# Whole units in place of half units between the steps of three recurrent mixer chains

## The reference

```python
mod = silu(c) @ ada_w + ada_b                       # six modulation rows of 1024 for each of 9 sequences
h = rms(x) * norm1_w * (1 + sc1) + sh1
proj = h @ w_in                                     # q/k/v/gates of four mixers, then merge gates
A: gated DeltaNet   # causal conv, l2 norm, per tile a triangular solve, 4 heads of 64
B: HGRN2            # per-channel decay, 4 heads of 64
C: Mamba-2 SSD      # causal conv, 8 heads of 32
D: mLSTM            # stabilised, 4 heads of 64
merged = sum_n sigmoid(gate_n) * (rms(mixer_n) * act(z_n)) @ w_branch[n]
x = x + gt1 * (merged @ w_out)
x = x + gt2 * swiglu(rms(x) * norm2_w * (1 + sc2) + sh2)
y = rms(x) * final_norm_w
```

## Time and profile before

| | |
|---|---|
| median of three runs | 1401.7 us (1396.46 to 1403.82) |
| the profiled execution | 1398.09 us, span 1396.3 us |
| PE busy | 1290.7 us, 92% |
| DVE busy | 633.8 us, 45% |
| ACT busy | 381.6 us, 27% |
| mean granted TensorE clock | 0.951 |
| HBM, mean over the span | 83 GB/s |

### The profile page before, as it was taken

The page is one execution under the profiler, slowest core; times in us unless marked ns, Lnnn a source line. Parts: engine busy times, 40 slices in busy tenths (PEclk is TensorE's granted clock), DMA queues, the critical chain, the costliest instruction groups (busy, mean ns, idle before and its releaser), DMA issues. The chain is left out here.

```text
span 1396.3 us, 23271 instructions
## 1 busy us (share of the span) xinstructions
PE 1290.7 (92%) x9849; PEld 1150.7 (82%) x9849; DVE 633.8 (45%) x1240; ACT 381.6 (27%) x561; POOL 12.0 (1%) x30
## 2 busy tenths in 40 slices
PE   5599989999988988999899999996999999989997
PEld 3478768678776766669899999895999999989996
DVE  1341753478788866444433333546222222263332
ACT  1421361552212211034521212114223222251112
POOL 0000100000000000000000000000000000000000
PEclk9799999999999977689999999997999999999999
DMA  9603622222120203025933222231322333223301
GB/s 315 213 16 89 112 92 91 92 91 76 42 66 3 91 1 91 2 67 92 207 85 76 76 76 76 76 85 37 90 81 77 83 90 90 62 83 84 84 22 65
DMA packets 191020, 116.79 MB, mean 84 GB/s; under 512 B 36650, under 2 KB 189351, under 8 KB 190678
## 3 DMA queue, kind: packets, MB, share of 16 engines
q1 hardware_dynamic: 190358, 115.42, 30.0%
q0 software_dynamic: 576, 0.14, 0.1%
HBM read 108.57 MB, written 6.96 MB: 83 GB/s over the span
## 5 line engine op out<-in xcount | busy, mean ns | idle before, releaser
L707 PE MATMUL ps<-scr_parts 128*128 128x272 f32 x2688 | 521.5, 293 | 16.1 <-DVE hT_parts L2213 8.2
L707 PEld LDWEIGHTS ps<-scr_parts 128*128 128x128 f32 x2688 | 429.5, 191 | 20.1 <-issue 13.3
L707 PE MATMUL ps<-hT_parts,scr_parts 128*128 128x272 f32 x1408 | 391.3, 291 | 0.0
L2115 DVE TENSOR_TENSOR scr_parts<-ring,scr_parts 128x1024 fp32r<-128x1024 f32 (+1 forms) x100 | 128.9, 1289 | 305.5 <-ACT scr_parts L1432 302.7
L707 PEld LDWEIGHTS ps<-hT_parts,scr_parts 128*128 128x128 f32 x1408 | 261.8, 190 | 0.0
L707 PE MATMUL ps<-hT,ring 128*128 128x272 f32 x960 | 247.3, 412 | 1.4 <-ACT pj L1306 1.4
L1432 ACT ACTIVATE scr_parts<-ring 128x1024 fp32r<-128x1024 f32 (+1 forms) x100 | 111.0, 1111 | 489.1 <-PE ps L707 488.4
L707 PEld LDWEIGHTS ps<-hT,ring 128*128 128x128 f32 x960 | 185.8, 199 | 43.4 <-issue 4.1
L707 PE MATMUL ps<-pj_parts,scr_parts 128*128 128x272 f32 x992 | 168.1, 294 | 5.7 <-DVEq L1559 5.7
L707 PE MATMUL ps<-scr 128*128 128x128 f32 (+11 forms) x1288 | 138.2, 300 | 14.5 <-DVEq L1559 7.9
L707 PEld LDWEIGHTS ps<-pj_parts,scr_parts 128*128 128x128 f32 x992 | 142.1, 191 | 7.2 <-DVEq L1559 6.3
(11 more groups left out here) (301 smaller groups left out, 1105.8 us busy)
## 6 DMA issues: line engine op xcount, KB each, us to landing
ring<-in_w_in_dram SPq DMA_DIRECT2D x62, 512.0 KB, 6.8
ring<-in_ada_w_dram SPq DMA_DIRECT2D x48, 512.0 KB, 6.5
ring<-in_ffn_w_in_dram SPq DMA_DIRECT2D x44, 512.0 KB, 5.0
ring<-in_ffn_w_out_dram SPq DMA_DIRECT2D x16, 384.0 KB, 3.6
ring<-in_ffn_w_out_dram SPq DMA_DIRECT2D x16, 320.0 KB, 4.1
ring<-in_w_out_dram SPq DMA_DIRECT2D x8, 512.0 KB, 5.0
x_scratch<-scr SPq DMA_DIRECT2D x1, 2176.0 KB, 13.6
Q<-x_scratch SPq DMA_DIRECT2D x1, 2176.0 KB, 10.8
```

Source lines behind the costliest of these rows:

```text
L707: return pe.matmul(out, lhsT, rhs, start=start, stop=stop, skip_group_check=True)
L2115: dve.tensor_tensor(lo, src, hi.bitcast(F32), SUB).then_inc(w_split, 1)
```

## The change

Units are issued whole. The planner gives PE one `product` per unit, with a planned length of 3.7 us for `mix`, 2.1 us for `ada` and 0.9 us for `turn`, and `unit_product(u)` issues all its instructions in a row. The instructions and their waits are the same ones; their order among the steps of the chains is another.

```diff
-                best = (start, "x", unit, f"part{part_}", "pe")
+                best = (start, "x", unit, "product", "pe")
...
-            free[eng] = start + {"mix": 1.85, "ada": 0.9, "turn": 0.9}[SEQUENCE[t][0]]
-            if part_ == 1:
-                evac.append((free[eng], unit))
-                unit, part_ = unit + 1, 0
-            else:
-                part_ = 1
+            free[eng] = start + {"mix": 3.7, "ada": 2.1, "turn": 0.9}[SEQUENCE[t][0]]
+            evac.append((free[eng], unit))
+            unit += 1
...
-            def unit_part(u, part_):
-
-                if part_ == 0 and u >= 2:
+            def unit_product(u):
+
+                if u >= 2:
 
                     pe.wait_ge(x_read, u - 1)
                 kind, v = SEQUENCE[u]
                 if kind == "mix":
                     n, c, h = load_of[("mixer", v // 4)], v // 2 % 2, v % 2
-                    if part_ == 0:
-                        landed(pe, n % R, n)
-                    for k in range(4 * part_, 4 * part_ + 4):
+                    landed(pe, n % R, n)
+                    for k in range(KD):
...
                 elif kind == "ada":
-                    n = load_of[("ada2", 2 * v + part_)]
-                    landed(pe, n % R, n)
-                    last = ada_rows_of(ps[:, u % 2, part_ * 256:(part_ + 1) * 256], n % R)
-                elif part_ == 1:
+                    for e in range(2):
+                        n = load_of[("ada2", 2 * v + e)]
+                        landed(pe, n % R, n)
+                        last = ada_rows_of(ps[:, u % 2, e * 256:(e + 1) * 256], n % R)
+                else:
 
                     pe.wait_ge(x_read, POS[("ada", v)] + 1)
                     for c in range(4):
                         last = mm(ps[:, u % 2, c * 9:(c + 1) * 9], rstd[:, c * P:(c + 1) * P], sum_groups)
-                if part_ == 1:
-                    last.then_inc(x_done, 1)
+                last.then_inc(x_done, 1)
...
-                    unit_part(t, int(name[-1]))
+                    unit_product(t)
```

More of the change, by code:

```diff
@@ L229, in shared_order @@
     ready = {c: 0.0 for c in chains}
-    out, unit, part_, evac = [], 0, 0, []
+    out, unit, evac = [], 0, []
     left = {c: sum(cost(name, eng) + 0.1 for _, name, eng in stages) for c, stages in chains.items()}
```

## The result

The changed kernel takes 1404.0 us (median of 12 runs, 1402.31 to 1408.76), the kernel before 1398.6 us (12 runs, 1396.4 to 1404.38): a ratio of 1.0036, with a 95% interval of 1.002 to 1.0052. It is slower by 5 us. The profiled execution took 1404.93 us with a span of 1403.1 us, 6.8 us over that of before.

The account below looks back on a forecast made before the run. The mixer stage was taken as an account of PE: unit and chain work, idle time and lower clock. Terms 38.2 - 18.6 - 19 - 5 - 3 - 2 + 7 gave -2.4 us, so 1399.3 us against the median; 8-in-10 range 1383 to 1421 us.

Parts of the forecast that it names:

- The point where the units end: Mixer stage: at 1.35 times the units per tile, the 76th unit comes 0.7 through tile 3, about 495 us.
- the units run out early: Rival, chance 0.25: at factor 1.5 the last unit is issued at 443 us of the old trace; +15 us, 1417 us.
- 38.2: Term: unit work from 500 to 605 us and the last block is pulled in front of the old 500 us mark, +38.2 us.
- Signs: Wrong if units remain behind the last chain step, end before 470 us, or DVE is under 70% without units.
- DVE's pace without units: Term for 500 to 605 us without units: DVE at 76% makes the stretch 86 us, -19 us.
- The seven waits of 30.6 us: In 500 to 605 us: DVE waited for PE, 7.7 down to 1.5 us, partly behind a unit's half; supported the 76%.
- Clock: Term: the end stage without units has more short idle times and a lower PE clock; 0 to +23 us, taken as +7.
- Idle time in 209 to 500 us: Term: whole units cover part of PE's 17.3 us idle time there; 0 to -17 us, taken as -5.
- The waits near 180 us: Term at 175 to 185 us: a whole unit covers PE's three waits for ScalarE's q and k normalisation, 5.3 us; taken as -3.
- The last block: Term at the mixer stage's end: the ten half units behind the last chain step go, -18.6 us.
- joints: Term: some 30 joints of halves standing alone, before the units run out, are saved; 0 to -5 us, taken as -2.
- The faster rival: Chance 0.25: at factor 1.2 units last until 562 us and the chains keep their pace; about -16 us, 1385 us.

Follow-up runs that it names:

- e3: Kernel before with units 0 to 39 in halves and units 40 to 75 whole: 1404.1 us, ratio 1.0033 to the kernel before.
- e6: Kernel before with units 0 to 59 whole and units 60 to 75 in halves: 1389.4 us, ratio 0.9941 to the kernel before.
- e2: Kernel before with units 0 to 39 whole and units 40 to 75 in halves: 1381.0 us, ratio 0.987 to the kernel before.
- e11: Kernel before with units 0 to 51 whole and the others in halves: 1383.0 us, ratio 0.9893 to the kernel before.
- e8: Changed kernel plus 30 short products, results unread, in planned PE holes behind the last unit: 1400.8 us, ratio 1.0008 to the kernel before.
- e9: Kernel before with only units 20 to 27 whole, all others in halves: 1396.9 us, ratio 0.999 to the kernel before.
- e10: Kernel before with only units 28 to 39 whole, all others in halves: 1390.0 us, ratio 0.9959 to the kernel before.
- e12: Kernel before with units 0 to 31 whole and the others in halves: 1385.1 us, ratio 0.99 to the kernel before.
- e7: Changed kernel, but a unit is placed only where PE would be free over 1.0 us: 1423.9 us, ratio 1.0179 to the kernel before.
- e16: Kernel before with units 0 to 39 whole, the others in halves, and the planner's weight for remaining chain work 0.004 instead of 0.003: 1391.7 us.
- e15: Kernel before with units 0 to 39 whole, the others in halves, and the planner's weight for remaining chain work 0.002 instead of 0.003: 1385.1 us.
- e14: Kernel before, all units in halves, with the planner's weight for remaining chain work 0.004 instead of 0.003: 1397.4 us.
- e1: Kernel before, units in halves, with the changed kernel's planned lengths for modulation units and turns: 1396.8 us, ratio 0.9986 to the kernel before.
- e5: Kernel before with units 0 to 15 whole and all others in halves: 1401.7 us, ratio 1.0022 to the kernel before.
- e13: Kernel before, all units in halves, with the planner's weight for remaining chain work 0.002 instead of 0.003: 1396.4 us.
- e4: Kernel before with mixer units in four quarters, modulation units and turns still in halves: 1409.1 us, ratio 1.0064 to the kernel before.

## Why the prediction was wrong, by its own steps

The direction failed: 2.4 us faster was forecast, 5 us slower was measured, inside the stated range.

- **The point where the units end is the step that failed.** The prediction kept 25 units in front of tile 0 of the delta rule, took 1.35 times as many per tile behind that, and spread them evenly over tile 3. So it put the end of the units at 495 us of the old time scale. The changed order, worked out from the code, has 28 units in front of tile 0; between the steps of the q and k normalisation, for one, a whole unit now stands where a half did. In tiles 0 to 2 it has 19, 13 and 13 units, up to the last PE step of each tile, where 14, 11.5 and 8 stood (the prediction counted 7.5 in tile 2): 1.34 times in all, so the factor itself held. At the end of tile 2 73 units are through and not 69.5, and 3 of these 3.5 come from in front of tile 0. Even so, at 9.5 units per tile, the last three would have reached to about 459 us. They all stand in front of the fourth PE step of tile 3: unit 75 comes behind the third, which the old trace has at 441.5 us, with 129 of 198 chain steps issued.
- **The rival "the units run out early"** is what happened: the loss without units shows in e3, e6 and all whole, and nothing is lost where they last (e2, e11). That it named 443 us is partly luck, as its factor of 1.5 per tile was not reached. It had a chance of 0.25 and a time of 1417 us, 13 us too high: +15 us where 5 were measured. The old trace, split at the point where the changed order runs out, shows where:

```profile
75.00:441.50 366.50, 345.48 (x2700) 278.57 (x2698) 226.01 (x538) 120.50 (x203) 9.31 (x18) 0.99 0.26 73
441.50:626.10 184.60, 161.35 (x1387) 121.66 (x1387) 118.17 (x289) 32.63 (x75) 0.00 (x0) 0.80 0.16 44
```

  The part in front grew by 44.4 us, to 410.9; the rival's terms say 43.2 (38.2 + 15 - 5 - 3 - 2). The part behind shrank by 37.9 us, to 146.7, and the rival's terms say only 28.6 (-18.6 - 19 - 2 + 7 + 4). DVE had done 14.1 us more of the chains' work in front (240.1 against 226.0 us), because other chains were further on (in the order, HGRN2 is four PE steps further in its tile 2 at that point). That was in no term.
- **Signs.** Of its own signs of being wrong one showed plainly, the end of the units before 470 us, and one was missed narrowly (DVE at 70.6% behind the units, where under 70% was the sign and 75% was hoped for). From 209 us to the end of the units PE was busy 264.6 of 276.9 us, 96% where 97% was asked, and DVE 171.4 us, 62% where 50 to 60% was said.
- **DVE's pace without units.** DVE was taken to be busy 76% of that stretch; it was 70.6% (103.5 of 146.7 us). At 76% the stretch would have been 136 us, 10.5 us shorter. The seven waits of 30.6 us that the forecast leaned on are the seven largest groups, 12 waits in all.
- **Clock.** The prediction added 7 us. The uncovered 147 us ran at 0.67, and e8 was 3 us (medians, not clear of noise) to 6 us (profiles) faster with products that serve no other end. No run had that stretch at the full clock, so the size of this term stays open.
- **Idle time in 209 to 500 us** fell from 17.3 to 15.2 us, by 2 us and not by 5.
- **The waits near 180 us.** PE's idle time in 75 to 209 us fell from 9.9 to 3.2 us, more than the 3 us taken. One wait of 3.2 us for ScalarE is left of three. But e9 shows that this is not to be had by making only those units whole.
- **The last block** went, as forecast, for 18.6 us. The loads caused no wait of PE; DMA moved more in 209 to 300 us (105 against 81 GB/s).
- **A term that was missing.** Whole units around tile 0 are a gain in themselves, 8 us for 28 to 39 alone (e10), 12 to 17 us for 0 to 31, 0 to 51 and 0 to 39 (e12, e11, e2). The sum had only small terms for joints and idle time. The faster rival had this sign, for another reason: its condition, units that last almost to the end, did not hold.
- **Rule of the Trainium skill.** The section "Optimization Strategy" of "Perfetto Trace Analysis" says that interleaving regimes with different bounds may help. The runs agree: e11, with units to the end, is 1.4% faster by the ratios than all units whole, which leave nothing to interleave at the end, where DVE is busy 71% and PE 74% of the time.

Two things stay open. No run had whole units beyond the 52nd that lasted to the end without holes left open for them (e7 brought a cost of its own). So a cost of late whole units by themselves is not told apart from that of running out; up to unit 51 there is none (e11).

And why whole units gain early is only argued. In e2 and e10 the HGRN2 chain is 13 to 20 us ahead at its tile 0, while the delta rule's tile 0 ends 21 us later, at about 293 us. So three chains run side by side sooner, and in e2 the end of the stage shows less idle time and a higher clock. The traces of all kernels whose units last to the end line up by that one time, with quarters (e4) and e7 at its far end:

```
run                        e2      e16     e11     e15     e10     e12     e14     e1
HGRN2's tile 0 ends (us)   336.1   338.2   338.4   340.5   342.3   345.4   350.5   355.3
median (us)                1381.0  1391.7  1383.0  1385.1  1390.0  1385.1  1397.4  1396.8

run                        before  e5      e9      e13     e4      e7
HGRN2's tile 0 ends (us)   355.7   356.2   357.7   358.5   366.4   371.0
median (us)                1398.6  1401.7  1396.9  1396.4  1409.1  1423.9
```

All six that end it before 346 us take 1381 to 1392 us, the six between 350 and 359 us take 1396 to 1402 us, and the two behind 366 us are the slowest. In the changed kernel it ends at 344.7 us, so it had this lead too and lost it at the end. No run moved that chain alone, so the lead may be a sign of the gain and not its cause.

## What to carry to other kernels

When filler work shares an engine with dependent chains, the size of a piece sets when the filler runs out. Ask where the last piece lands in the chain's own progress, because everything behind it runs with holes, here at a mean clock of 0.67. Do not trust a count per stretch that is spread evenly: 3 more units in front of the first tile, and 3 bunched at the start of another, moved the end of the units by some 50 us here. Coarse pieces early and fine ones late (40 whole units, then halves) beat both uniform choices at all three weights of the planner, by 6 to 17 us against halves; holding filler back for larger holes (e7) was the worst of all. Before a difference of 0.5% between two hand-planned orders is explained, draw the order again with a neighbouring parameter: here that moved one and the same grain by up to 11 us.

## What the runs showed of the hardware

Adding useless products to a stretch in which the chains set the pace made it shorter in the profiles. 30 products, 14 us of PE work at full clock, raised the mean granted clock of that stretch from 0.67 to 0.80, and it took 140.9 us in place of 146.7. In the medians 3.2 us are left of that, with overlapping intervals, so it is an indication that such work can pay for itself and no proof. That TensorE's clock falls to 1.2 GHz behind idle time was in the trace of before, behind 3.90 us of idle time; before that gap the clock was 1.00:

```profile
500.00:504.00 4.00, 4.00 (x49) 3.34 (x48) 3.33 (x8) 1.23 (x3) 0.00 (x0) 1.00 0.00 0
510.00:520.00 10.00, 10.00 (x66) 7.47 (x64) 4.17 (x13) 1.04 (x3) 0.00 (x0) 0.50 0.01 2
```
